# Third buffers, a sum one round ahead and down weights by row blocks in the ConvFFN of a hybrid decoder step

## The reference, cut to what matters

```
def conv_ffn(xn, buf, w_up, w_conv, b_conv, w_down):     # xn 544 x 1024, D_FF = 2816
    u, gt = jnp.split(xn @ w_up, 2, axis=-1)
    up = jnp.concatenate([buf, u], axis=1)
    conv = b_conv + sum(w_conv[j] * up[:, j:j + t] for j in range(3))
    y = (jax.nn.silu(conv) * gt) @ w_down
...
a_out, m_out of the two head groups -> w_out;  m_out = sigmoid(m_o) * norm(h) * mlstm_norm_g
x = x + g2 * f
```

## Time and profile before

| | before |
|---|---|
| median of 3 runs | 1691.96 us (1686.0 to 1702.23) |
| the profiled execution | 1694.95 us, its span 1693.2 us |
| TensorE busy | 1591.4 us, 94% of the span |
| VectorE, ScalarE, GpSimd busy | 61%, 43%, 18% |
| chain that ended last | TensorE 66%, DMA 14%, VectorE 8%, ScalarE 4% |
| seven-product rounds and their down projections | about 530 to 835 us (layer 0) and 1357 to 1662 us (layer 1) |

### The profile page before, as it was taken

How to read it: one execution, slowest core, us unless ns; L and a number is a source line. 1 busy time by engine, 2 the same in 40 slices (tenths; PEclk the granted TensorE clock), 3 DMA queues, 4 the chain that set the end, 5 groups by cost and what they waited for, 6 DMA issues and landing times.

```text
span 1693.2 us, 37537 instructions
## 1 busy us (share of the span) xinstructions
PE 1591.4 (94%) x14375; PEld 1432.9 (85%) x14375; DVE 1038.8 (61%) x2518; ACT 724.9 (43%) x1585; POOL 306.5 (18%) x434
## 2 busy tenths in 40 slices
PE   6999999988999999999989999998799999999997
PEld 5899975557999999999989997645689999999997
DVE  3544446657487867758564354575656877768765
ACT  3322237634243734536342213664333444635434
POOL 1011104422102212212001101252210121212111
PEclk9999999999999999999999999999999999999999
DMA  9435297369516958766133536634845486858632
GB/s 344 136 91 186 67 366 251 118 198 180 190 60 144 215 146 181 174 158 142 54 103 92 185 116 237 224 91 151 165 78 168 96 212 148 193 153 177 168 76 65
DMA packets 234898, 266.76 MB, mean 158 GB/s; under 512 B 16074, under 2 KB 176266, under 8 KB 234268
## 3 DMA queue, kind: packets, MB, share of 16 engines
q1 hardware_dynamic: 209088, 210.90, 40.9%
q0 software_dynamic: 25632, 53.47, 16.6%
HBM read 218.21 MB, written 16.68 MB: 139 GB/s over the span
## 4 chain that ended last, share of the span: by engine, by line
PE 66%; DMA 14%; DVE 8%; ACT 4%; issue 4%; DVEq 1%; SPq 1%; POOL 1%; ACTq 1%; POOLq 0%
PE ps L1745 13%; PE ps L1120 13%; DMA slab<-slab 11%; PE ps L1609 8%; PE ps L1550 5%; PE ps L963 3%; PE ps L1598 2%; PE ps L1259 2%; PE ps L1244 2%; PE ps L1171 2%; DMA slab<-in_w_out 2%; PE ps L1104 2%; PE ps L1582 1%; PE ps L1115 1%; PE ps L1114 1%
## 5 line engine op out<-in xcount | busy, mean ns | idle before, releaser
L3439 POOL DMA_DIRECT2D slab<-slab x144 | 125.2, 904 | 586.1 <-DMA slab<-in_w_up 154.4
L1120 PE MATMUL ps<-slab_r,work_r 128*128 128x256 f32 x960 | 205.6, 282 | 0.0
L1120 PEld LDWEIGHTS ps<-slab_r,work_r 128*128 128x128 f32 x960 | 157.8, 188 | 2.7 <-issue 2.5
L1745 PE MATMUL ps<-side_r,big_r 128*128 128x272 f32 x672 | 140.6, 290 | 5.6 <-DVE xT L3027 2.9
L1745 PE MATMUL ps<-side_r,slab_r 128*128 128x272 f32 x672 | 139.0, 288 | 0.0
L1745 PE MATMUL ps<-big_r 128*128 128x272 f32 x672 | 138.6, 288 | 0.0
L1609 PE MATMUL ps<-big_r,slab_r 128*128 128x272 f32 x432 | 101.5, 296 | 16.0 <-ACT xnT L2230 9.4
L1745 PEld LDWEIGHTS ps<-side_r,big_r 128*128 128x128 f32 x672 | 105.4, 188 | 8.3 <-DVE xT L3027 3.8
L2461 DVE TENSOR_TENSOR slab_r<-slab,big_r 128x1024 fp32r<-128x1024 f32 (+1 forms) x68 | 90.4, 1348 | 25.6 <-ACT big_r L2196 16.3
L1745 PEld LDWEIGHTS ps<-big_r 128*128 128x128 f32 x672 | 105.6, 189 | 0.0
L1609 PE MATMUL ps<-work_r,more_weights_r 128*128 128x272 f32 x432 | 104.6, 295 | 0.6 <-ACT xnT L2230 0.3
(11 more groups left out here) (556 smaller groups left out, 4499.5 us busy)
## 6 DMA issues: line engine op xcount, KB each, us to landing
slab<-in_w_up SPq DMA_DIRECT2D x180, 256.0 KB, 3.5
slab<-in_w_mod SPq DMA_DIRECT2D x22, 2048.0 KB, 10.9
slab<-slab POOLq DMA_DIRECT2D x144, 256.0 KB, 4.7
slab<-in_w_in SPq DMA_DIRECT2D x20, 1024.0 KB, 5.7
slab<-in_w_down SPq DMA_DIRECT2D x20, 1024.0 KB, 7.7
slab<-in_cache_cmp_kv SPq DMA_DIRECT2D x128, 128.0 KB, 2.0
slab<-in_cache_sel_kv SPq DMA_DIRECT2D x96, 128.0 KB, 2.0
big<-in_cache_win_kv SPq DMA_DIRECT2D x16, 512.0 KB, 7.7
```

Of the source, the lines that this page charges most:

```text
L1120: ins = mm(ps[n % 4][:, 0:cw], x, fr(wt[:, k, :]), start=k == 0 and m == 0, stop=k == KC - 1 and m == 2)
L1745: ins = mm(ps[bank + b][:, 0:HALF], wt, fr(x[:, k, HALF * b:HALF * b + HALF]), start=k == 0 and n == 0, stop=k == n_k - 1 and n == 2)
L3439: pool.dma_start(block_of(kind, c), src, accum_op=ALU.add).then_inc(sums_in[kind], 16)
```

## The change

Four edits, all in the ConvFFN stage and its surroundings.

1. M5's and M7's blocks get a third buffer. M7's is a new piece of 512 columns of more_weights; M5's is rows_bc[:, 0:512], which until then holds the layer's head gains. load_g1 and load_third wait for block c-3 in place of c-2 and are issued four blocks ahead. The head gains of layer 1 are loaded after the last fourth_sum of layer 0. On GpSimd third_sum runs two blocks ahead, and first_sum(c+1) comes right behind second_sum(c).
2. The scratch for DMA descriptors falls from 8 KB to 4 KB a partition.
3. On ScalarE the down highs come between the high of M7 and the high of M6.
4. load_down loads single row blocks, one DMA each, each waiting for the landing of the one before: blocks 0 and 1 of a group where the two halves were issued, block 2 at the end of SyncE's step c = 4g+1 and block 3 at the end of step 4g+2. Each down high waits for its own row block.

```diff
-        more = sb_both("more_weights", [128, 2048])
+        more = sb_both("more_weights", [128, 2560])
...
-                return piece(slab[0], 1 + c % 2)
+                i = (c - CL) % 3
+                return piece(slab[0], 1 + i) if i < 2 else piece(more, 4)
+            if kind == "M5":
+                i = (c - CL) % 3
+                return piece(slab[2], 4 + i) if i < 2 else rows_bc[:, 0:512]
...
                 def load_g1(c):
-                    if c >= CL + 2:
-                        sp.wait_ge(*sum_at("M6", c - 2, L))
-                        sp.wait_ge(*low_at("M5", c - 2, L))
+                    if c == CL + 2:
+                        sp.wait_ge(mo_g.sem, mo_g.at(1, L))
+                    if c >= CL + 3:
+                        sp.wait_ge(*sum_at("M6", c - 3, L))
+                        sp.wait_ge(*low_at("M5", c - 3, L))
...
                 def load_third(c):
-                    if c >= CL + 2:
-                        sp.wait_ge(*low_at("M7", c - 2, L))
+                    if c >= CL + 3:
+                        sp.wait_ge(*low_at("M7", c - 3, L))
...
-                def load_down(j):
-                    n = 2 if j < NG else 1
-                    load("ffn", 1, down_copies(lambda k: slice(4 * j + k, 4 * j + k + n), n), j)
+                def load_down(j, ks):
+                    if 0 in ks:
+                        load("ffn", 1, [], j)
+                    for k in ks:
+                        if 4 * j + k < FC:
+                            if k:
+                                sp.wait_ge(*down_loaded(j, k - 1, L))
+                            sp.dma_start(slab[1][:, D * k:D * k + D], wdn[L, :, 4 * j + k, :]).then_inc(down_in, 16)
...
-                load_down(0)
+                load_down(0, range(4))
...
                 load_third(CL + 2)
+                load_g1(CL + 3)
+                load_third(CL + 3)
                 load_u(CL + 2)
-                load_down(1)
+                load_down(1, (0, 1))
                 for c in range(CL, FC - 1):
+                    if c + 4 < FC:
+                        load_g1(c + 4)
+                        load_third(c + 4)
                     if c + 3 < FC:
-                        load_g1(c + 3)
-                        load_third(c + 3)
                         load_g2(c + 3)
                         load_u(c + 3)
                     if c % 4 == 0 and c > CL:
-                        load_down(c // 4)
+                        load_down(c // 4, (0, 1))
+                    elif c % 4 in (1, 2):
+                        load_down(c // 4, (c % 4 + 1,))
...
-                def split_down(part, n_k):
+                def split_down(part, n_k, j):
+                    act.wait_ge(*down_loaded(j, part, L))
...
                     if more_up:
                         high("M7", c + 1)
+                    for part in ((), (0, 1), (2,), (3,))[q] if g < NG else ():
+                        split_down(part, 1, g)
+                    if more_up:
                         high("M6", c + 1)
-                    if g < NG:
-                        if q == 1:
-                            act.wait_ge(slab_in[1], slab_loads("ffn", 1, L, g))
-                        for part in ((), (0, 1), (2,), (3,))[q]:
-                            split_down(part, 1)
                     silu(1, c)
...
                 third_sum(CL)
                 first_sum(CL)
+                third_sum(CL + 1)
                 for c in range(CL, FC):
                     second_sum(c)
                     if c + 1 < FC:
-                        third_sum(c + 1)
+                        first_sum(c + 1)
                     fourth_sum(c)
-                    if c + 1 < FC:
-                        first_sum(c + 1)
+                    if c + 2 < FC:
+                        third_sum(c + 2)
+                if L + 1 < DEPTH:
+                    pool.wait_ge(*low_at("M5", FC - 1, L))
+                    load_head_gains(L + 1)
...
-    nc = _bacc.Bacc("TRN2", target_bir_lowering=False, num_devices=1, dynamic_dma_scratch_size=8192)
+    nc = _bacc.Bacc("TRN2", target_bir_lowering=False, num_devices=1, dynamic_dma_scratch_size=4096)
```

More of the change, by code:

```diff
@@ L345, in block_of @@
             if kind == "M7":
-                return piece(slab[0], 1 + c % 2)
-            return piece(slab[2], {"M1": 0, "M6": 0, "M2": 2, "M3": 2, "M5": 4}[kind] + c % 2)
+                i = (c - CL) % 3
[3 more added lines that the diff above has]
+                return piece(slab[2], 4 + i) if i < 2 else rows_bc[:, 0:512]
+            return piece(slab[2], {"M1": 0, "M6": 0, "M2": 2, "M3": 2}[kind] + c % 2)
         part_hi = {"M1": work[:, 9984:10496], "M2": big[:, 0:512], "M5": up[:, 0, 0:512], "M6": piece(slab[0], 4),
@@ L440, in trunk_program @@
             dmas[s] += {0: 1, 2: 2}[s] * (FC - CL)
+        dmas[1] -= PARTS["ffn"] * 6
         slab_in = [ctx.enter_context(nc.semaphore(f"slab{s}_loaded")) for s in range(NSLAB)]
@@ L639, in low_at, with down_loaded @@
             return b_lo.sem, b_lo.at(n + 1 + (4 if n >= 2 else 0), L)
+        down_in = ctx.enter_context(nc.semaphore("down_row_blocks_loaded"))
+        def down_loaded(j, k, L):
+            return down_in, 16 * (L * (4 * NG + 2) + 4 * j + k + 1)
         g1_in, third_in = [ctx.enter_context(nc.semaphore(n)) for n in ("gate_first_blocks_loaded", "sum_3_first_terms_loaded")]
@@ L810, in up_copies @@
                     return [(dst[:, :, h, :], wup[L, :, :, h, q]) for h in range(2)]
-                def down_copies(row, n):
-                    dst = slab[1][:, 0:2 * n * D].rearrange("p (k n) -> p k n", n=D)
-                    return [(dst[:, n * i:n * i + n, :], wdn[L, :, row(n * i), :]) for i in range(2)]
                 def load_block(dst, h, k, c, sem):
@@ L2264, in _ @@
                     split_h(q, q)
-                    if q == 1:
-                        act.wait_ge(slab_in[1], slab_loads("ffn", 1, L))
                     for k in ((), (0, 1), (2, 3), ())[q]:
-                        split_down(k, 1)
+                        split_down(k, 1, 0)
                 product1_out(CL)
@@ L2302, in _ @@
                     if not more_up:
-                        act.wait_ge(slab_in[1], slab_loads("ffn", 16, L))
                         for part in range(2):
-                            split_down(part, 1)
+                            split_down(part, 1, NG)
                     product5_out(c)
@@ L3322, in _, with load_head_gains @@
                 pool.dma_start(dst, src).then_inc(rows_in, 16)
+            def load_head_gains(L):
+                pool.dma_start(rows_bc[:, 0:512], A["mlstm_norm_g"][L, :].partition_broadcast(128),
+                               allow_slow_non_contiguous=True).then_inc(bc_in, 16)
             def load_gains(L):
-                for dst, src in ((rows_bc[:, 0:512], A["mlstm_norm_g"][L, :].partition_broadcast(128)),
-                                 (rows_bc[:, 512:520], A["b_if"][L, :].partition_broadcast(128)),
+                for dst, src in ((rows_bc[:, 512:520], A["b_if"][L, :].partition_broadcast(128)),
                                  (m0s[:, :], A["state_mlstm_m"][L, :, :].rearrange("b h -> h b"))):
                     pool.dma_start(dst, src, allow_slow_non_contiguous=True).then_inc(bc_in, 16)
+            load_head_gains(0)
             load_gains(0)
```

## The result

The changed kernel takes **1733.3 us** (median of 6 runs, 1726.8 to 1739.5) against 1690.4 us (6 runs, 1686.0 to 1702.2): a ratio of 1.0237, 95% interval 1.0204 to 1.0269. It is slower by 2.4%, where 1712 us had been forecast. Its profiled execution took 1728.7 us.

The account below looks back on a forecast made before the run. TensorE, busy 94% of the span, was taken as the bound, with only its waits and lower clock to win. 33.6 + 6.4 + 0.7 - 21.0 = +19.7 us gave 1712 us, range 1674 to 1736.

Parts of the forecast that it names:

- The sign and the mechanism: Slower kernel: ScalarE waits 2 to 4 us for late down blocks, sixteen times, and TensorE about 2 us at M6.
- rival C: Heavy waits at M6 for late blocks: 8 x 6.0 = 48 us plus clock 12.8, total 1732.5 us; chance 0.15.
- rival A: Blocks 2 and 3 land in time, no queue ahead; all 21.0 us won less 0.7, total 1671.7; chance 0.15.
- Gain, 21.0: Up-projection stretches: better-timed weights win 16.3 us of TensorE waits and 4.7 us of lower clock.
- the 10.9 us that I booked to the row blocks: Block 6, both layers: two long waits and their lower clock go, 3.5 + 1.6 and 2.7 + 3.1 us.
- Blocks 0 and 1, start of the stage: First down blocks, loaded one after the other, some 20 us beside up weights: hidden before their first copy.
- The last pair, 0.7: Last two down blocks: the second lands some 0.35 us late per layer, 0.7 us in all.
- Scratch 0: 4 KB of DMA scratch, at the decode-state DMAs: costs 0, at most 2 us per layer.
- head gains 0: Head gains loaded behind the sums, 256 KB once, wanted by the next layer's gate sums: costs 0.
- Landing of blocks 2 and 3: Behind the up loads: block 2 lands at 642.0, ScalarE waits 3.0 us; TensorE waits 2.3 + 1.9, 33.6 in all.
- My upper bound: Latest landing of block 2, under sums: 642.9, with waits of 3.2 + 2.8 us.
- The clock, 6.4: Clock falls hidden after a pair's first M6 wait, 1.6 us after the second; half counted: 8 x 1.6 / 2.

Follow-up runs that it names:

- e3_halves: The changed kernel with the old two 1 MB down loads a group in place of single row blocks: 1672.3 us beside 1694.4 for the kernel before, ratio 0.9863.
- e9_rows: The kernel before with only the down weights loaded by single row blocks: 1735.5 us beside 1695.2 for the kernel before, ratio 1.0230.
- e8_old_order: e3_halves with GpSimd's old order of sums, third buffers kept: 1689.0 us beside 1692.8 for the kernel before, ratio 0.9984.
- e5_scratch: The kernel before with only the DMA scratch cut from 8 to 4 KB: 1695.4 us beside 1692.8, ratio 1.0014.
- e4_ahead_of_up: The changed kernel with blocks 2 and 3 issued on M3's low but ahead of the two up loads: 1686.8 us beside 1694.4 for the kernel before, ratio 0.9940.
- e11_four_free: e3_halves with four 512 KB row blocks issued together, none waiting for another, in place of two 1 MB loads: 1672.2 us, ratio 0.9872 to the kernel before.

## Why the prediction was off, by its own steps

The sign and the mechanism were right: sixteen waits of ScalarE for late row blocks, TensorE late at M6 of blocks 7, 8, 11, 12 and so on, the second sum waiting for VectorE, the first sum of block 6 in 4.8 us:

```profile
L3459 POOL DMA_DIRECT2D rows_bc<-slab x1: 1207/1207/1207, 535.5 to 535.5; - x1
...
DMA to landing us min/median/max: 4.8/4.8/4.8
```

The size was not: 1733 where 1712 was forecast, inside the range and next to rival C's 1732.5, which had been given 0.15. C's terms, 48 + 12.8 us, are nearer to what was measured (41.3 + 13.6) than the forecast's 33.6 + 6.4. The range was drawn from 1674 up, though rival A, meant to be its lower end, stood at 1671.7.

Term by term, on the stretches:

- **Gain, 21.0:** right in size, 20.6 in e3_halves. I took the long waits of block 6 to go because the 9 us transfers shrink. That is one way, and e9_rows shows that it works alone (0.53 and 0.97 us). It isn't needed: in e3_halves they go while these transfers take 10.1 and 12.3 us, as first_sum(6) leaves ahead of them. Nor is the sums' order needed at M6 itself: e8_old_order waits 0.28 us there, but 1.0 and 2.0 us for M3 in that round and the next (layer 0). So the 10.9 us that I booked to the row blocks come without them too.
- **Blocks 0 and 1, start of the stage:** hidden, as held; no split waits there. **The last pair, 0.7:** ScalarE waited 0.74 and 0.11 us, TensorE 1.01 and 0.38 where it had stood 0.15 each before: 1.1. **Scratch 0, head gains 0:** right (e5_scratch, and nothing missing in e3_halves).
- **Landing of blocks 2 and 3: the step that failed.** I had 5.7 us from issue to landing (636.3 to 642.0) and measured 5.8 to 7.8, median 7.2. I had put the block right behind the up load with its own data, 1.4 us, on top. The up load came as forecast (5.6 us after issue). The block came 2.7 us behind it, in company of three sums of 256 KB that left in the same 2 us. My upper bound, from the 539 stretch where sums and down weights met, had been 642.9, or 6.6 us; that was the row to take, and even it is 0.6 short of the median. The rest of the chain was right: the split to M6's low took 4.1 us. So ScalarE's first waits are 4.45 us on average (3.0 forecast), TensorE's 3.53 (2.3). The second ones are 1.63 on TensorE (1.9), on a ScalarE wait of 2.6. All pairs: 8 x 5.16 = 41.3 for 33.6.
- **The clock, 6.4:** 13.6. Seven of the eight first waits (3.2 to 4.4 us) have a fall at their end, two of 6.8 us and five of 3.4, 30.7 us at half the clock, of which 3.5 still lie in the waits: (30.7 - 3.5) / 2 = 13.6. The first wait of 3.01 us has none, nor have the second ones. I had them the other way round. That a fall after a first wait is hidden by the next M6 is partly true: the second waits are 1.05 and 1.12 us behind the falls of 6.8 and 3.29 behind the first wait without one, so it seems that most of the 2.6 and 2.9 us lost in those falls was had back, as a shorter second wait. That rests on three pairs.
- **Sum:** 41.3 + 1.1 + 13.6 = 56.0 of cost for 40.7 forecast; 59.7 measured against e3_halves, so 3.7 us are in no term. With the gain of 20.6 that makes +39.1 for +19.7. The execution gained 5.4 us outside the stretches. No term explains that; e3_halves gained 3.4 there, and two executions of its kernel differ by 7.0.

The page "DMA: Bandwidth & Descriptors" of the Trainium skill: its fit, which the section "Anatomy of one DMA — SWDGE (gpsimd) path" gives for DMAs issued by GpSimd, makes 3.2 us for 512 KB. In this trace that holds for a row block issued by SyncE with nothing beside it (3.2 us, the one issued at 841.1), and it would have missed the late ones by 4 us. Its rule of ring order, in the section "Queues, rings and completion order", agrees with e4_ahead_of_up: ahead of the up loads the blocks land in 3.8 to 6.2 us. The same section says that a completion's increment lands only after every earlier write of that DMA engine, across its queues, which would tie a load to sums on GpSimd's queue; the block and the sum issued 0.07 us after it landed within 0.2 us of each other, but no run here separates that from shared bandwidth. And its section "Bandwidth" asks for DMAs of 1 MiB or more: here four of 512 KB were as good as two of 1 MB (1672.2 and 1671.2 us).

Open stays how the 7.2 us divide between the up loads ahead and the sums beside: e4_ahead_of_up moves the block away from both at once, by some 1.3 us in time as well.

## What to carry to other kernels

When a load is moved to a later event, price its landing by the busiest stretch in which its neighbours were seen together, not by its bytes behind the last load (here 6.6 against 5.7 us, with 7.2 measured); then price the clock behind every wait that this makes longer than those the trace already shows without a fall. A wait for a landing on the engine that issues loads costs what is queued behind it, so let the consumer wait, not the issuer. And take the parts of a mixed change apart: here the sums a round ahead with the highs' order win 1.4%, the row blocks lose 2.3% alone and 3.8% on top of the other edits, and e3_halves is the kernel to keep.

## What the runs showed of the hardware

- Four DMAs of 512 KB issued together were all in 12.3 us after the first was issued, in the first group of e11_four_free; two of 1 MB took 13.0 in e3_halves. The time of the kernel was the same (ratios 0.9872 and 0.9856).
- In the changed kernel the same 512 KB took 3.2 us alone and up to 7.8 us behind up loads and beside sums.
- Half the dynamic DMA scratch (4 KB) cost nothing that can be told from noise: 1.0014, interval 0.9990 to 1.0038.
- A wait's length alone doesn't tell whether the clock falls to 1.2 GHz. In the changed kernel it fell at seven waits of 3.2 to 4.4 us and at none of 0.3 to 3.3 (granted clock 1.00 over 1411 to 1430, with the waits of 3.01 and 3.29). With the row blocks alone (e9_rows) it fell at or just behind eight waits of 2.1 to 4.0 us, among them 2.1, 2.6 and 2.7, and not at four of 2.9 to 3.2.
